# Expert gates of a routed feed-forward stage: selection rows read weighted, or read plain and multiplied with the affinities

## The reference, cut to what matters

```python
def expert_choice_ffn(h, w_router, w_g, w_u, w_d):
    cap = CAPACITY_FACTOR * n // N_EXPERTS        # 64 of 512, or 32 of 256 tokens for each of 16 experts
    logits = jnp.einsum('bnd,de->ben', h, w_router)
    aff = jax.nn.softmax(logits, axis=1)
    gate, idx = lax.top_k(aff, cap)
    xs = h[bi, idx]
    a = jnp.einsum('becd,edf->becf', xs, w_g)
    u = jnp.einsum('becd,edf->becf', xs, w_u)
    y = jnp.einsum('becf,efd->becd', jax.nn.silu(a) * u, w_d)
    return jnp.zeros_like(h).at[bi, idx].add(y * gate[..., None])
```

## Time and profile before

| | |
|---|---|
| three runs | 3881.96, 3884.84, 3885.41 us, median 3884.84 |
| profiled execution | 3885.41 us, its span 3883.6 us |
| busy share of the span | PE 90%, PEld 60%, DVE 32%, ACT 26%, POOL 5% |
| mean granted clock of TensorE | 0.961 of full speed |
| layer 0's experts | from 1098 us to about 1660 us |
| layer 1's experts | from 2378 us to about 2877 us |

### The profile page before, as it was taken

The page is one execution under the profiler, slowest core; times in us unless marked ns, Lnnn a source line. Parts: engine busy times, 40 slices in busy tenths (PEclk is TensorE's granted clock), DMA queues, the critical chain, the costliest instruction groups (busy, mean ns, idle before and its releaser), DMA issues.

```text
span 3883.6 us, 47860 instructions
## 1 busy us (share of the span) xinstructions
PE 3511.1 (90%) x21214; PEld 2340.0 (60%) x21218; DVE 1232.5 (32%) x1685; ACT 1023.7 (26%) x1639; POOL 200.3 (5%) x124
## 2 busy tenths in 40 slices
PE   7998889999799999989889988788879888989998
PEld 5786556767653443467658874222237754867886
DVE  3235641112421110144663342111133334344333
ACT  3524431112310000045453231000021335333222
POOL 0100000111200000001000120000001010020000
PEclk9999999999799999999999988999999999999999
DMA  6440003442169999822003325999962010323331
GB/s 212 130 125 17 1 12 119 128 133 71 55 254 387 355 344 397 313 43 81 23 1 82 98 98 203 409 409 409 409 227 65 20 45 17 98 65 92 92 98 49
DMA packets 359981, 600.82 MB, mean 155 GB/s; under 512 B 48770, under 2 KB 242656, under 8 KB 359520
## 3 DMA queue, kind: packets, MB, share of 16 engines
q1 hardware_dynamic: 357024, 596.69, 43.5%
q10 hardware_dynamic: 2752, 1.08, 0.1%
HBM read 595.62 MB, written 2.10 MB: 154 GB/s over the span
## 4 chain that ended last, share of the span: by engine, by line
PE 73%; DVE 10%; DMA 7%; ACT 6%; SPq 3%; issue 1%; POOL 0%; ACTq 0%; POOLq 0%; DVEq 0%
PE ps L557 30%; PE ps L1791 6%; PE ps L2133 5%; DMA ring<-in_w_e_down 3%; DMA ring<-in_w_e_up 3%; PE ps L1283 3%; PE ps L606 3%; SPq L2435 3%; PE ps L1823 3%; PE ps L1794 3%; DVE sm L1047 3%; ACT tmp L1065 3%; PE ps L577 2%; DVE tmp L1080 2%; PE ps L1038 2%; PE ps L1471 2%
## 5 line engine op out<-in xcount | busy, mean ns | idle before, releaser
L557 PE MATMUL ps<-xh,wh 128*128 128x512 f32 x1912 | 648.0, 377 | 39.6 <-DVE xl L1993 17.6
L557 PE MATMUL ps<-xl,wh 128*128 128x512 f32 x1912 | 633.9, 370 | 0.0
L557 PE MATMUL ps<-xh,wl 128*128 128x512 f32 x1912 | 632.5, 369 | 0.0
L532 DVE TENSOR_TENSOR wl<-ring,wh 128x1024 fp32r<-128x1024 f32 (+1 forms) x247 | 309.6, 1255 | 475.8 <-ACT wh L523 475.7
L557 PEld LDWEIGHTS ps<-xh,wh 128*128 128x128 f32 x1912 | 331.1, 190 | 130.2 <-issue 51.7
L523 ACT ACTIVATE wh<-ring 128x1024 fp32r<-128x1024 f32 (+1 forms) x247 | 258.9, 1049 | 431.6 <-PE ps L557 171.4
L557 PEld LDWEIGHTS ps<-xh,wl 128*128 128x128 f32 x1912 | 332.0, 190 | 62.5
L557 PEld LDWEIGHTS ps<-xl,wh 128*128 128x128 f32 x1912 | 331.1, 190 | 62.5 <-issue 4.3
L1791 PE MATMUL ps<-ring,arena 128*32 128x512 f32 x2048 | 267.3, 593 | 1.0 <-DVE arena L1573 1.0
L1786 PE MATMUL ps<-ring,arena 128*64 128x512 f32 x1024 | 235.1, 598 | 30.7 <-DMA ring<-in_w_e_up 16.7
L1092 PE MATMUL ps<-consts,tmp 128*128 128x128 f32 x832 | 127.6, 286 | 70.1 <-DVE arena L1149 55.2
(11 more groups left out here) (246 smaller groups left out, 4465.9 us busy)
## 6 DMA issues: line engine op xcount, KB each, us to landing
ring<-in_w_e_gate SPq DMA_DIRECT2D x128, 1024.0 KB, 10.8
ring<-in_w_e_up SPq DMA_DIRECT2D x128, 1024.0 KB, 10.8
ring<-in_w_e_down SPq DMA_DIRECT2D x128, 1024.0 KB, 14.2
ring<-in_w_in SPq DMA_DIRECT2D x116, 512.0 KB, 4.2
ring<-in_w_ada SPq DMA_DIRECT2D x96, 512.0 KB, 5.6
ring<-in_w_ff SPq DMA_DIRECT2D x64, 512.0 KB, 4.0
ring<-in_w_out SPq DMA_DIRECT2D x24, 512.0 KB, 4.1
ring<-in_w_in SPq DMA_DIRECT2D x40, 256.0 KB, 4.0
```

The source lines that it names most:

```text
L532: e.tensor_tensor(m.WL[:, o:o + many], halves.aps[s][:, 0:many], m.WH[:, o:o + many].bitcast(F32), ALU.subtract).then_inc(*lo.up(X.key, q))
L557: i = e.matmul(ps[0:M, a:b], w[:, k, 0:M], h[:, k, a:b], start=k == 0 and p == 0, stop=k == 7 and p == 2)
```

## The change

The rounds transpose the plain 0/1 selection. ACT copies each round once, straight into `GX` or `GC`. The multiplications with the affinities, the `is_gt` operations and the sums are gone. In their place a further round comes last (round 6 in layer 0, round 4 in layer 1): for each pair of experts the selection is the stationary operand, in 128 x 128 blocks, and the two columns of affinities of the pair are the moving operand. There are 4 matmuls for each of 8 pairs, and in layer 0 2 more for each pair for the context. VectorE then copies the halves that belong to each expert out of `P3` into `gate`. `pe_flip` of expert 0 waits for these copies, since it writes into `P3`; the back product waits for ACT's last copy, where it waited for VectorE; `act_outer` waits for the gates, and ACT's first `act_silu` of layer 0 no longer waits for VectorE. The eight operations of VectorE that zero halves of `yc` in layer 0 (L1694) stay behind the gates.

```diff
         def pe_round(e, l, r):
...
-            e.wait_ge(*d_lz.at(st, "times", r))
...
-                                        SXG[:, c, 4 * r + 2 * g:4 * r + 2 * g + 2, :].rearrange("p e c -> p (e c)"), ident)
-            else:
+                                        SXf[:, c, 4 * r + 2 * g:4 * r + 2 * g + 2, :].rearrange("p e c -> p (e c)"), ident)
+            elif r < last_round(l):
+                e.wait_ge(*r_dve.at(st, "sd", 1))
...
+            else:
+                for g in range(MANY):
+                    for c in range(4):
+                        i = e.matmul(P3[:, 2 * g:2 * g + 2], SXf[:, c, 2 * g:2 * g + 2, :].rearrange("p e c -> p (e c)"),
+                                     affT[:, c, 2 * g:2 * g + 2], start=g == 0 and c == 0, stop=c == 3, skip_group_check=True)
+                    for c in range(0 if l else 2):
+                        i = e.matmul(P3[:, 512 + 2 * g:514 + 2 * g], SCf[:, c, g].rearrange("p r e c -> p (r e c)"),
+                                     affT[:, 4 + c, 2 * g:2 * g + 2], start=g == 0 and c == 0, stop=c == 1, skip_group_check=True)
             i.then_inc(*p_lz.up(st, r))

         def act_round(e, l, r):
             st = f"e{l}"
             e.wait_ge(*p_lz.at(st, r))
-            if r == 5:
-                e.wait_ge(*d_lz.at(st, "one", 4))
-            n = 512 if r < 4 else 256
-            for g in range(1024 // n):
...
             if r < 4:
+                e.activation(GX[:, 2 * r:2 * r + 2, :].rearrange("p g t -> p (g t)"), P3[:, :], ACT.Copy).then_inc(*c_lz.up(st, r))
+            elif r < last_round(l):
+                e.activation(MO[0].GC[:, 4 * r - 16:4 * r - 12, :].rearrange("p g t -> p (g t)"), P3[:, :], ACT.Copy).then_inc(*c_lz.up(st, r))

         def dve_gates(e, l):
             st = f"e{l}"
...
-            dve_times(e, l, 0)
-            dve_times(e, l, 1)
-            for r in range(n):
-                if r + 2 < n:
-                    dve_times(e, l, r + 2)
-                dve_one(e, l, r)
+            e.wait_ge(*p_lz.at(st, last_round(l)))
+            pairs = lambda o: P3[:, o:o + 16].rearrange("p (g e) -> p e g", e=2)
+            for x in (0, 1):
+                e.tensor_copy(gate[64 * x:64 * x + 64, 0:8], pairs(0)[64 * x:64 * x + 64, x]).then_inc(*d_lz.up(st, "x", x))
+            for x in range(0 if l else 4):
+                e.tensor_copy(gate[32 * x:32 * x + 32, 8:16], pairs(512)[32 * x:32 * x + 32, x % 2]).then_inc(*d_lz.up(st, "c", x))
...
         def pe_flip(e, l, x):
...
-                e.wait_ge(*c_lz.at(st, last_round(l) - 1))
+                e.wait_ge(*d_lz.at(st, "x", 1))
+                if l == 0:
+                    e.wait_ge(*d_lz.at(st, "c", 3))
...
-                    if x == 0 and 0 < 2 * k2 + w <= last_round(l):
+                    if x == 0 and 0 < 2 * k2 + w <= last_round(l) + 1:
                         pe_round(e, l, 2 * k2 + w - 1)
```

More of the change, by code:

```diff
@@ L367, in build @@
                                (("sx", 6144, 4096), ("sc", 10240, 2048), ("y0", 6144, 2048), ("y1", 8192, 2048), ("yc0", 10240, 2048)))
[L368 to L371, removed]
+        gx = nc.alloc_sbuf_tensor_at("gx", [128, 4096], F32R, offset=tmp_at)
         SX, SXf = (sx[:, :].bitcast(t).rearrange("p (t e c) -> p t e c", t=4, e=16) for t in (F32R, F32))
         SC, SCf = (sc[:, :].bitcast(t).rearrange("p (t g r e c) -> p t g r e c", t=2, g=8, r=2, e=2) for t in (F32R, F32))
-        GX, GXG = (t[:, :].rearrange("p (g t) -> p g t", g=8) for t in (gx, gxg))
+        GX = gx[:, :].rearrange("p (g t) -> p g t", g=8)
         YX = [[y[:, 1024 * j:1024 * j + 1024] for j in (0, 1)] for y in (y0, y1)]
@@ L1624, in back_depth @@
             return 2 if l == 0 else 3
-        HG = tmp[:, 4096:5120]
         def pe_round(e, l, r):
@@ L1643, in pe_round @@
                         i = e.transpose(P3[:, 256 * g + 128 * c:256 * g + 128 * c + 128],
-                                        SCG[:, c, 4 * r - 16 + g].rearrange("p r e c -> p (r e c)"), ident)
+                                        SCf[:, c, 4 * r - 16 + g].rearrange("p r e c -> p (r e c)"), ident)
+            else:
[6 more added lines that the diff above has]
+                                     affT[:, 4 + c, 2 * g:2 * g + 2], start=g == 0 and c == 0, stop=c == 1, skip_group_check=True)
             i.then_inc(*p_lz.up(st, r))
@@ L1649, in act_round @@
             e.wait_ge(*p_lz.at(st, r))
-            if r == 5:
-                e.wait_ge(*d_lz.at(st, "one", 4))
-            n = 512 if r < 4 else 256
-            for g in range(1024 // n):
-                dst, col = (GXG[:, 2 * r + g, :], 2 * r + g) if r < 4 else (HG[:, 256 * g:256 * g + 256], 8 + 4 * r - 16 + g)
-                e.activation(dst, P3[:, n * g:n * g + n], ACT.Copy, accum_out=gate[:, col:col + 1]).then_inc(
-                    *c_lz.up(st, *((r,) if n * g + n == 1024 else (r, g))))
@@ L1658, in dve_times @@
-        def dve_times(e, l, r):
-            st = f"e{l}"
-            if r < 4:
[L1661 to L1680, removed]
+            if r < 4:
+                e.activation(GX[:, 2 * r:2 * r + 2, :].rearrange("p g t -> p (g t)"), P3[:, :], ACT.Copy).then_inc(*c_lz.up(st, r))
+            elif r < last_round(l):
+                e.activation(MO[0].GC[:, 4 * r - 16:4 * r - 12, :].rearrange("p g t -> p (g t)"), P3[:, :], ACT.Copy).then_inc(*c_lz.up(st, r))
@@ L1682, in dve_gates @@
         def dve_gates(e, l):
             st = f"e{l}"
-            n = last_round(l)
-            dve_times(e, l, 0)
-            dve_times(e, l, 1)
-            for r in range(n):
-                if r + 2 < n:
-                    dve_times(e, l, r + 2)
-                dve_one(e, l, r)
+            e.wait_ge(*p_lz.at(st, last_round(l)))
+            pairs = lambda o: P3[:, o:o + 16].rearrange("p (g e) -> p e g", e=2)
+            for x in (0, 1):
+                e.tensor_copy(gate[64 * x:64 * x + 64, 0:8], pairs(0)[64 * x:64 * x + 64, x]).then_inc(*d_lz.up(st, "x", x))
@@ L1695, in dve_gates, with gates_made @@
                                         ALU.mult).then_inc(*d_lz.up(st, "zero", t, j, x))
+        def gates_made(l):
+            return d_lz.at(f"e{l}", *(("x", 1) if l else ("c", 3)))
         def pe_back(e, l, p, norm=None):
@@ L1705, in pe_back @@
             e.wait_ge(*e_st.at(st, p))
-            e.wait_ge(*d_lz.at(st, "one", last_round(l) - 1))
+            e.wait_ge(*c_lz.at(st, last_round(l) - 1))
             if l == 0:
@@ L1857, in act_silu @@
             n = 3 if l else 2
-            if l == 0 and x == 0:
-                e.wait_ge(*d_lz.at(st, "one", last_round(l) - 1))
             if x >= n:
@@ L1878, in act_outer @@
             e.wait_ge(*e_dn.at(st, p, 3))
+            e.wait_ge(*gates_made(l))
             e.activation(YX[p % 2][0], ps[:, :], ACT.Copy, scale=gate[:, p:p + 1]).then_inc(*e_y.up(st, p))
```

## The result

The changed kernel is slower: 3910.49 us median (3902.24 to 3916.53) against 3885.12 (3881.96 to 3886.15), a ratio of 1.0065, 95% interval 1.0042 to 1.0088. Its profiled execution took 3911.86 us with a span of 3910.1, that is 26.5 us over the span of before. The forecast was 3908.8 us, 24.0 over the median of 3884.8 that it started from.

A forecast was written before the change was run, and what follows sets the result against it. TensorE was taken to bound layer 0's experts and DMA loads layer 1's. Removed work saves 0; 17.8 us in layer 0 plus 6.2 in layer 1 make 24.0, so 3908.8 us, range 3896 to 3918 us.

The forecast's parts named there:

- What bounds the stages: Experts' stages: layer 0 lasts as long as TensorE's program, layer 1 as its DMA loads at 412 GB/s.
- What is removed saves 0: Both layers' rounds: VectorE and ScalarE work removed is off the chain, saving 0; upper bound 4.4 us.
- The price of an instruction: Added matmuls, two instruction pairs each: 0.107 to 0.128 us per instruction at full clock, 0.213 at half.
- The step that took the low rate from a product with 16 columns for one with 2: Added matmuls: the router's 0.213 us should change little with 2 columns, because the weight load sets the pace.
- Which clock: Both layers' added matmuls: clock falls part way, half charged at either level; chance 0.62, against 0.25 that it holds.
- layer 0, the pass: Layer 0's 96 added instructions, half at each clock level: 15.4 us, all on the chain.
- layer 0, slow stretch behind it: Layer 0, thick work after the added matmuls runs about 5 us at half speed, costing about 2.4 us.
- layer 1, the pass: Layer 1's 64 added instructions behind expert 0's sixth group, half at each clock level: 10.2 us of delay.
- layer 1, slowed group: Layer 1, the group following the added matmuls is slowed, adding about 1 us of delay.
- layer 1, slack: Layer 1, the tenth load may be issued as late as 2400.3 us without loss, a slack of 5.0 us.
- layer 1, loss: Layer 1, delay of 11.2 us less 5.0 slack: 6.2 us lost, none given back by the load-bound stage.
- The cover of VectorE's copies: Layer 0: VectorE done at 1147 us, before flip 0 at 1154, so hidden; without cover about 5 us.

The follow-up runs named there:

- without the pass: Changed kernel with only the first expert pair's matmuls left in the last round, other gates not computed; 3884.25 us median against 3883.3, ratio 1.0002.
- fp32r: Changed kernel with affinities split into high and low fp32r parts, one instruction pair per matmul with four columns, VectorE adding the parts; 3890.37 us median, ratio 1.0013.
- 64 columns: Changed kernel with 64 columns streamed through each weight load in place of 2, same matmul count and result; 3899.3 us median, ratio 1.0039.
- changed kernel again: The changed kernel measured and profiled a second time, with no edit; 3906.26 us median, ratio 1.0053.
- pass twice: Changed kernel with the two loops over expert pairs run twice in both layers, same result; 3939.09 us in one execution.

## Why the prediction was right, by its own steps

**What bounds the stages** held: TensorE alone in layer 0, the loads in layer 1. **What is removed saves 0** held (run without the pass); the busy times of VectorE and ScalarE fell by 15.9 and 3.0 us, less than the 20 and 5 forecast, with no effect on the time. VectorE's eight gate copies of about 0.16 us make up 1.3 us of its difference; what makes up the rest was not looked for.

**The price of an instruction** was 0.112 us at full clock, between the ends of 0.107 and 0.128, and 0.213 at half, the router's value, whose clock was 0.50 too. The step that took the low rate from a product with 16 columns for one with 2, since the load sets the pace, was right: 16 and 2 columns both cost 0.213 us at a clock of 0.50, 2 and 64 both 0.112 us at 1.00.

**Which clock** was the largest guess, with 0.62 on it, and right in both profiles of the changed kernel. That it falls half way had no row behind it, and here luck helped. By the spacings, about 43 of the 96 instructions of layer 0 ran at full clock, which is near half, and about 46 of the 64 of layer 1, which is not: that pass was forecast 1.2 us too long. Work without a gap did not keep the clock up: it fell from 1.00 to 0.50 in both profiles with no idle time of TensorE, and stayed at 0.50 for 33 us in the run with two passes.

**The sums**, against the first profile:

| term | forecast, us | measured, us |
|---|---|---|
| layer 0, the pass | 15.4 | 16.1 |
| layer 0, slow stretch behind it | 2.4 | 2.9 |
| layer 1, the pass | 10.2 | 9.0 |
| layer 1, slowed group | 1.0 | 1.7 |
| layer 1, slack | 5.0 | 4.0 |
| layer 1, loss | 6.2 | 6.7 |
| sum | 24.0 | 25.7 of 26.5 |

Every term has the right sign and size within 1.2 us, and part of the closeness is luck: in layer 1 the pass was put 1.2 us too long, the slowed group 0.7 too short and the slack 1.0 too large, which leaves 0.5. For each run, how much later than 1.72 us the tenth load follows the ninth, and layer 1's loss against 499.72 us:

| run | delay, us | loss, us | difference |
|---|---|---|---|
| without the pass | 1.1 | 0.1 | |
| fp32r | 3.8 | 0.0 | |
| 64 columns | 7.4 | 2.7 | 4.7 |
| changed kernel | 10.65 | 6.7 | 4.0 |
| changed kernel again | 10.66 | 6.7 | 4.0 |
| pass twice | 24.8 | 20.6 | 4.2 |

The ninth and the tenth load's issue with fp32r, and with 64 columns:

```profile
2395.27 0.37 SPq L2424 DMA_DIRECT2D ring<-in_w_e_up  x1
2400.80 0.37 SPq L2424 DMA_DIRECT2D ring<-in_w_e_gate  x1
```

```profile
2407.74 0.37 SPq L2414 DMA_DIRECT2D ring<-in_w_e_up  x1
2416.89 0.37 SPq L2414 DMA_DIRECT2D ring<-in_w_e_gate  x1
```

Nothing is lost up to 3.8 us of delay; beyond that the loss is the delay less 4.0 to 4.7 us. This is the dry queue, as the forecast had it, with a smaller slack than its 5.0. **The cover of VectorE's copies** held: they and the first products ended at 1147.9 us in the changed kernel, and flip 0 started at 1155.3.

Open: what exactly makes the clock fall where it does within a pass, how many columns between 2 and 64 would keep it up, and what makes the executions of the changed kernel spread over 14 us.

## What to carry to other kernels

Where one engine alone sets the end, work that is moved onto it from idle engines costs its full price, however small its arithmetic: here a matmul instruction with two columns cost its weight load, 0.112 us for 128 columns of fp32 and 0.213 once the clock had fallen. In a stage bound by loads, ask which load each delay holds back and how long the queue can go without it: the same pass, 9 to 10 us of TensorE, cost 6.7 us in one place and nothing ten groups later. Exact 0/1 matrices can be copied to bf16 before they become weights: the pass of layer 0 went from 16.1 to 1.3 us, though the kernel as a whole was then only as fast as before the change.

## What the runs showed of the hardware

- In the pass the granted clock fell from 1.00 to 0.50 while TensorE had no gap and loaded 128 columns of weights for each 2 streamed (1.00 from 1125.85 to 1130.70 us, then 0.50, with PE and PEld busy for 9.00 of 9.00 us). With 64 streamed, at the same 0.112 us from start to start, it stayed at 1.00 through the pass.
- With fp32r weights matmul instructions followed each other no faster than with fp32, 0.112 us from start to start at full clock with four and two columns; with bf16 ones they took about 0.027 us with six columns behind each, four times as fast.
